# Attention up-projections from one weight chunk, and two output tiles taken together at the start of a stage

## The reference, cut to what matters

```python
def _mixer_mla(b, q_norm_g, w_uq, kv_norm_g, w_ukv, pos):
    c_q, c_kv, k_rope = jnp.split(b, [256, 384], axis=-1)           # latents: 256, 128, rope 32
    q = (_rms_norm(c_q, q_norm_g) @ w_uq).reshape(B, S, 4, 96)      # 4 heads, 64 + 32
    kv = (_rms_norm(c_kv, kv_norm_g) @ w_ukv).reshape(B, S, 4, 128) # keys 64, values 64
    ...                                                             # rope, softmax attention

def second_block(x, ...):
    for l in range(2):
        x = _layer_norm(alpha * x + 0.5 * _swiglu(x, ...), ...)
        x = _layer_norm(alpha * x + _token_mixers(x, ...), ...)     # window, MLA, axial, differential
        x = _layer_norm(alpha * x + 0.5 * _swiglu(x, ...), ...)
    return x
```

## Time and profile before

| | us |
|---|---|
| median of 3 runs (3507.78 to 3513.71) | 3512.36 |
| the profiled execution, its own time | 3510.07 |
| its span, first to last instruction | 3508.3 |
| TensorE busy | 3367.8 |
| VectorE busy | 1803.3 |
| ScalarE busy | 1411.4 |
| mean granted TensorE clock, of full | 0.977 |

### The profile page before, as it was taken

The page is one execution under the profiler, slowest core; times in us unless marked ns, Lnnn a source line. Parts: engine busy times, 40 slices in busy tenths (PEclk is TensorE's granted clock), DMA queues, the critical chain, the costliest instruction groups (busy, mean ns, idle before and its releaser), DMA issues.

```text
span 3508.3 us, 47079 instructions
## 1 busy us (share of the span) xinstructions
PE 3367.8 (96%) x17468; PEld 2774.4 (79%) x17468; DVE 1803.3 (51%) x2572; ACT 1411.4 (40%) x2167; POOL 12.7 (0%) x13
## 2 busy tenths in 40 slices
PE   7999999999999999999998999999999999899997
PEld 6898888888788888888865778888888866588886
DVE  5573566537766534333577553335333576563335
ACT  5323344326544324222456442224232457542223
POOL 0000000001000000000000000000000000000000
PEclk9999999999999999999999999999999999999998
DMA  3201232322232322222211122222223210122233
GB/s 130 67 31 37 80 102 96 99 95 93 76 102 96 99 95 95 97 97 95 76 43 35 43 78 96 98 97 89 96 96 99 80 52 28 35 76 96 96 98 102
DMA packets 89736, 288.48 MB, mean 82 GB/s; under 512 B 9968, under 2 KB 14576, under 8 KB 89072
## 3 DMA queue, kind: packets, MB, share of 16 engines
q1 hardware_dynamic: 89440, 284.69, 24.6%
q0 software_dynamic: 144, 1.71, 0.1%
HBM read 284.26 MB, written 2.10 MB: 82 GB/s over the span
## 4 chain that ended last, share of the span: by engine, by line
PE 84%; DVE 9%; ACT 4%; issue 3%; DMA 1%; DVEq 0%; ACTq 0%; SPq 0%
PE gb L583 24%; PE gb L584 24%; PE gb L585 24%; PE gb L1244 2%; DVE wl L2023 1%; PE pm L1257 1%; PE pm L1277 1%; DVE rinv L2053 1%; ACT wh L1405 1%; ACT h L1455 1%; DMA wst<-in_weights 1%; DVE h L2039 1%; DVE work_a L2656 1%; ACT work_a L1893 1%; ACT xh L1467 0%
## 5 line engine op out<-in xcount | busy, mean ns | idle before, releaser
L583 PE MATMUL gb<-xh,wh 128*128 128x512 f32 (+1 forms) x3168 | 1193.7, 377 | 59.7 <-DVE xl L2077 31.6
L584 PE MATMUL gb<-xl,wh 128*128 128x512 f32 (+1 forms) x3168 | 1169.9, 369 | 0.0
L585 PE MATMUL gb<-xh,wl 128*128 128x512 f32 (+1 forms) x3168 | 1169.8, 369 | 0.0
L2023 DVE TENSOR_TENSOR wl<-wst,wh 128x1024 fp32r<-128x1024 f32 (+3 forms) x600 | 646.5, 1091 | 447.3 <-ACT wh L1405 441.2
L1405 ACT CAST wh<-wst 128x1024 fp32r<-128x1024 f32 (+3 forms) x600 | 555.7, 942 | 604.4 <-DMA wst<-in_weights 604.2
L583 PEld LDWEIGHTS gb<-xh,wh 128*128 128x128 f32 x3168 | 605.7, 191 | 197.4 <-issue 49.9
L584 PEld LDWEIGHTS gb<-xl,wh 128*128 128x128 f32 x3168 | 607.2, 192 | 99.1 <-issue 4.9
L585 PEld LDWEIGHTS gb<-xh,wl 128*128 128x128 f32 x3168 | 606.6, 191 | 98.6
L583 PE MATMUL gb<-hid,wh 128*128 128x512 f32 (+2 forms) x1276 | 471.6, 370 | 10.3 <-DVE wl L2023 9.5
L585 PE MATMUL gb<-hid,wl 128*128 128x512 f32 (+2 forms) x1276 | 467.9, 367 | 0.0
L584 PE MATMUL gb<-hid,wh 128*128 128x512 f32 (+2 forms) x1276 | 467.8, 367 | 0.0
(11 more groups left out here) (401 smaller groups left out, 2989.9 us busy)
## 6 DMA issues: line engine op xcount, KB each, us to landing
wst<-in_weights SPq DMA_DIRECT2D x408, 512.0 KB, 3.3
wst<-in_weights SPq DMA_DIRECT2D x84, 384.0 KB, 3.0
wst<-in_weights SPq DMA_DIRECT2D x84, 320.0 KB, 2.9
h<-in_x_t SPq DMA_DIRECT2D x2, 1024.0 KB, 6.1
out_t<-h SPq DMA_DIRECT2D x8, 256.0 KB, 2.3
tab<-in_first SPq DMA_DIRECT2D x1, 1984.0 KB, 14.9
wst<-in_weights SPq DMA_DIRECT2D x20, 96.0 KB, 2.1
tab<-in_second POOLq DMA_DIRECT2D x1, 1666.0 KB, 7.3
```

The costliest lines, as they stand in the source:

```text
L583: pe.matmul(dst, w_hi, x_hi, start=start, stop=False)
L584: pe.matmul(dst, w_hi, x_lo, start=False, stop=False)
L585: return pe.matmul(dst, w_lo, x_hi, start=False, stop=stop)
L2023: dve.tensor_tensor(wl[:, s, m, a], wst[:, s, m, a], f32(wh[:, s, m, a]), ALU.subtract).then_inc(lo_split, 1)
```

## The change

Chunks 9 to 13 of each second-block mixer become one chunk 9 with 768 columns in half 0 (queries) and 512 in half 1 (keys and values), split at step 21. The output projection moves up to chunks 10 to 13; its first two chunks are split at steps 26 and 31. The parts of the up-projections stay at their steps, read the one chunk, and hand over through a new semaphore `lat_done` or, for the last reader of a half, through `half_done` and `chunk_done`. In `two_by_half` the two tiles of the first chunk are taken together in the first token half, and VectorE splits half 1 of the first chunk after j = 0 (`FIRST_AT`) in place of j = 1.

```diff
-UQ_COLS = (2 * 96, 2 * 96)
+LAT_COLS = (4 * 2 * 96, 4 * 64 + 2 * P)
-M0_C, LRU_C, M2_C = 20, 14, 18
+M0_C, LRU_C, M2_C = 20, 14, 14
+FIRST_AT = 0
-SPLIT_STEP = {0: 3, 3: 4, 6: 5, 10: 6, 14: 7, 18: 8, 21: 9, 24: 10, 25: 11, 27: 12, 28: 13, 30: 14, 32: 15}
+SPLIT_STEP = {0: 3, 3: 4, 6: 5, 10: 6, 14: 7, 18: 8, 21: 9, 26: 10, 31: 11}
...
-                stream(c0 + FF_C + 8, 2, (COLS, COLS), UQ_COLS)
-                stream(c0 + FF_C + 10, 4, UQ_COLS)
-                stream(c0 + FF_C + 14, 4)
+                stream(c0 + FF_C + 8, 2, (COLS, COLS), LAT_COLS)
+                stream(c0 + FF_C + 10, 4)
...
+                def two_tiles(v, s, m, j):
+                    t = HV[v]
+                    if s == 0 and m == 0:
+                        pe.wait_ge(xl_ready, 8 * n + 4 * v + j + 1)
+                    if v == 0 and j == 0:
+                        wait_half(c + s, m)
+                    for k in (2 * j, 2 * j + 1):
+                        col = slice(k * P, k * P + P)
+                        mm = three(gb[:, 2 * s + m, t], wh[:, s, m, col], wl[:, s, m, col], xh[:, k, t], xl[:, k, t],
+                                   k == 0, k == KT - 1)
+                    if v == 1 and j == KT // 2 - 1:
+                        mm.then_inc(chunk_done if m else half_done, 1)
+
+                together = (0, 0), (0, 1), (1, 0), (0, 2), (1, 1), (0, 3), (1, 2), (1, 3)
+                for v in range(2):
+                    for m, j in sorted(together) if v else together:
+                        two_tiles(v, 0, m, j)
+                        if v == 0 and m == 0 and j == 3 and not isinstance(ln_run, str):
+                            sums(n, ln_run, 1)
+                    for m in range(2):
+                        for j in range(KT // 2):
+                            two_tiles(v, 1, m, j)
...
                 def latent_part(c, i):
                     q("ml_lo", 3, 2 if c < 11 else 3)
                     for m in ((i,) if c < 11 else range(2)):
-                        wait_half(c0 + c, m)
+                        wait_half(c0 + 9, 0 if c < 11 else 1)
                         bank_free(c, m)
...
-                        mm.then_inc(chunk_done if m else half_done, 1)
+                        mm.then_inc(half_done if (c, m) == (10, 1) else S("lat_done"), 1)
...
-                        if v == 0 and first and j == 1:
+                        if v == 0 and first and j == FIRST_AT:
                             split_half(*first, 1)
```

More of the change, by code:

```diff
@@ L179, in pack_weights @@
         ukv = i["mla_w_ukv_2"][l].reshape(1, P, 4, 128)
[L180 to L184, removed]
+        up_kv = np.concatenate([ukv[0, :, :, :64].reshape(P, 256), ukv[0, :, :, 64:].reshape(P, 256)], 1)
+        put(uq.transpose(2, 0, 1, 3).reshape(8, P, 96), up_kv.reshape(P, 8, 64).transpose(1, 0, 2))
         w = i["w_out_2"][l].reshape(4, 4, 64, D)
@@ L1195, in latent_part @@
                         for k, f in enumerate(tiles):
-                            col = slice(k * width, k * width + width)
-                            mm = three(gb[0:width, m, :], wh[:, c % 2, m, col], wl[:, c % 2, m, col], *lat(f), k == 0, k == len(tiles) - 1)
-                        mm.then_inc(chunk_done if m else half_done, 1)
+                            at_ = (2 * (2 * (c - 9) + m) + k if c < 11 else 2 * (c - 11) + m) * width
+                            col, half = slice(at_, at_ + width), 0 if c < 11 else 1
+                            mm = three(gb[0:width, m, :], wh[:, 1, half, col], wl[:, 1, half, col], *lat(f), k == 0, k == len(tiles) - 1)
+                        mm.then_inc(half_done if (c, m) == (10, 1) else S("lat_done"), 1)
                 def latent_values(c, m):
-                    wait_half(c0 + c, m)
                     bank_free(c, 1)
+                    cols = slice(256 + P * m, 256 + P * m + P)
                     for t in range(NT):
@@ L1206, in latent_values @@
                         x_hi, x_lo = lat_tok(t)
[L1207 to L1210, removed]
+                        pe.matmul(dst, x_hi, wh[:, 1, 1, cols], start=True, stop=False)
+                        pe.matmul(dst, x_hi, wl[:, 1, 1, cols], start=False, stop=False)
+                        mm = pe.matmul(dst, x_lo, wh[:, 1, 1, cols], start=False, stop=True)
+                    mm.then_inc(chunk_done if m else S("lat_done"), 1)
                 def part_of(c, i):
@@ L1333, in out_part @@
                         for m in range(2):
-                            wait_half(c0 + 14, m)
+                            wait_half(c0 + 10, m)
                         q("exp_done", NS, NS - 1)
@@ L1372, in mixer2 @@
                 q("exp_done", NS, NS)
-                residual_out(c0 + 14, None, n, l, 2 + l, 1)
+                residual_out(c0 + 10, None, n, l, 2 + l, 1)
             def lat(k):
@@ L1473, in norm @@
                     high(j, 0)
-                    if first and j == 0:
+                    if first and j == FIRST_AT:
                         split_half(*first, 1)
@@ L1834, in split @@
                 def split(c):
-                    split_hi(c0 + c, c % 2, UQ_COLS if 9 <= c < 14 else (COLS, COLS))
+                    split_hi(c0 + c, c % 2, LAT_COLS if c == 9 else (COLS, COLS))
                 def evict(c, b):
@@ L1841, in evict @@
                     else:
-                        act.wait_ge(chunk_done if b or c == 13 else half_done, c0 + c + 1)
+                        if c < 9:
+                            act.wait_ge(chunk_done if b else half_done, c0 + c + 1)
+                        elif c == 13:
+                            act.wait_ge(chunk_done, c0 + 10)
+                        elif (c, b) == (10, 1):
+                            act.wait_ge(half_done, c0 + 10)
+                        else:
+                            q("lat_done", 8, 2 * (c - 9) + b + (1 if c < 11 else 0))
                     src = gb[:, 2 * (c == 1) + b, :]
@@ L1979, in mixer2 @@
                         split(SPLIT_STEP[u])
-                residual_out(c0 + 14, n, l, 1)
+                residual_out(c0 + 10, n, l, 1)
             act.wait_ge(S("ones_ready"), 1)
@@ L2633, in split @@
                 def split(c):
-                    split_lo(c0 + c, c % 2, UQ_COLS if 9 <= c < 14 else (COLS, COLS))
+                    split_lo(c0 + c, c % 2, LAT_COLS if c == 9 else (COLS, COLS))
                 def maxima(s):
@@ L2774, in mixer2 @@
                 assert m2.count == M2_STEPS, m2.count
[L2775 removed]
+                residual_out(c0 + 10, 6 + 3 * l, l, 1)
             dve.memset(one[:, :], 1.0)
@@ L2809, in _ @@
                 mixer2(l, c0 + FF_C, 2 + l)
-                norm(n + 1, l, late=(lambda: late_out(c0 + FF_C + 14, n + 1, l), lambda: tail_add(n + 1, 1)), first=(c0 + FF_C + M2_C, 0), split=next_split(c0 + FF_C + M2_C + 1))
+                norm(n + 1, l, late=(lambda: late_out(c0 + FF_C + 10, n + 1, l), lambda: tail_add(n + 1, 1)), first=(c0 + FF_C + M2_C, 0), split=next_split(c0 + FF_C + M2_C + 1))
                 ffn(c0 + FF_C + M2_C, g0 + FF_G + M2_G, 3 + 2 * l, n + 2, l, None)
```

## The result

| | before | after |
|---|---|---|
| median, us | 3512.20 (4 runs) | 3490.42 (3486.76 to 3493.01, 4 runs) |
| profiled execution, its own time | 3510.07 | 3490.86 |
| span | 3508.3 | 3489.1 |
| TensorE busy | 3367.8 | 3355.1 |
| span less TensorE busy | 140.5 | 134.0 |

The account below looks back on a forecast made before the run. TensorE, busy 96% of the span, bounds the kernel; only its idle time and the half clock behind can shrink. 17.6 plus 1.7 gives 19.3 us off 3510.07, 3490.8, put at 3492 against the median; 8-in-10 range 3482 to 3506.

Parts of the forecast that it names:

- Part one: Both second-block mixers: one latent chunk removes waits and half clock, net 8.8 us per layer, 17.6 for two.
- The wait of 4.19 us: Both mixers, part of chunk 12 waiting for its split: wait goes, 4.19 us, plus 3.9 of half clock behind it.
- the 2.71 us wait: Mixers, TensorE behind ScalarE's copy of a transposition, with an output chunk's split just ahead: the 2.71 us goes.
- The split at step 21: Mixers: wider latent halves end 1.4 us later on VectorE, all on TensorE; with 1.5 of half clock, 2.9 lost.
- The two waits ahead of step 28: Mixers, output split at step 26: TensorE waits 1.6 us for an eviction and 0.7 for a rotation, 2.3 lost.
- four waits of 0.3 to 0.6 us: Mixers, step 28 to 33: TensorE runs closer behind VectorE's maxima and ScalarE's copies, 1.8 us lost per layer.
- the stall only moves: Rival: output splits at steps 26 and 31 bring waits with half clock as before; time 3501 us, chance 0.18.
- Part two: Ten first-chunk stages: two tiles together and an earlier VectorE split fill TensorE waits, 1.7 us gained in all.
- The stages pinned to their second half: Five stages behind second-block layer norms: less cover makes a wait 1.4 us longer; 0.5 gained in each of four.
- the later half clock that I charged with 1.0 in all: Part two's stages: longer waits late in a stage bring half clock into TensorE-bound work, 1.0 us lost in all.
- The three stages with sums ahead: Stages at 1317, 2404, 3484 us: moved split delays the late add and sums 1.2 us; 0.3 charged each.
- The slower rival: First halves of ten stages: tile (0, 1) at half clock delays the sums up to 2.6 us; 3519 us, chance 0.06.

Follow-up runs that it names:

- together_rms: Changed kernel with tiles together and early split only in the four stages behind RMS norms, the others as before: 3493.20 us, 0.9939 to the kernel before.
- out_splits_late: Changed kernel with its first two output chunks split at steps 30 and 32 in place of 26 and 31: 3486.10 us, 0.9925 to the kernel before.
- chunk_alone: Changed kernel with the old tile order and VectorE's split of half 1 back after j = 1, leaving the merged latent chunk: 3497.20 us, 0.9956 to the kernel before.
- together_late_split: Changed kernel, tiles still together, with only VectorE's split of half 1 back after j = 1: 3485.45 us, 0.9927 to the kernel before.
- together_alone: Kernel before with two tiles together and the earlier split of half 1, its five latent chunks kept: 3500.81 us, 0.9968 to the kernel before.
- changed_again: Changed kernel, unedited, profiled and timed again: 3490.51 us, 0.9944 to the kernel before.
- latent_split_20: Changed kernel with the latent chunk split at step 20 in place of 21: 3479.06 us, 0.9913 to the kernel before.
- latent20_out24: Changed kernel with the latent chunk split at step 20 and the first output chunk at 24 instead of 26: 3477.65 us, 0.9896 to the kernel before.

## Why the prediction was right, and where its terms were off

**Part one, the mixers: right in mechanism and place, and in the net.** From step 20 to step 39 the sum said 8.8 us a layer; the profiles of the changed kernel show 8.6 to 8.7 four times. Of its single terms:
- The wait of 4.19 us and the half clock behind it went as listed; the 2.71 us wait became 0.82.
- The split at step 21 cost 1.42 us on TensorE, as worked out (1.4). The 1.5 us of half clock that I added for the 2.8 us wait did not come: the clock is 1.00 from 1868 to 1900. It can come: in together_rms the clock is 0.62 from 1868 to 1877, behind the same wait, and 1.3 us are lost by step 24.
- The two waits ahead of step 28 were placed right and sized at 2.3; measured 1.52 and 0.88. From step 28 on I took four waits of 0.3 to 0.6 us, 1.8 in all; the trace has 1.08, 0.79, 0.82, 1.13 and 0.72. This term is too small, and the absent half clock gives back what it loses, which is why the net agrees. That is partly luck.
- One reading was loose: the clock of 0.92 "before the 4.19 us wait" is a mean over 1895 to 1906, which takes in most of the wait. It is 1.00 from 1895 to 1904 and 0.58 from there to 1906, so the clock fell within the wait.
- The edits to the two output splits carry 3.4 of the 8.6 us; out_splits_late shows that.

**The rival "the stall only moves" is partly true, at times.** In chunk_alone's second mixer the same new waits were followed by half clock and the net fell to 5.56 us. In together_late_split it was 6.84 and 2.53, in together_rms 5.45 and 2.49. So the same edit gives 2.5 to 8.7 us a layer, by whether the clock falls behind the waits of 0.8 to 1.5 us at steps 26 to 29. The sum took one outcome for fixed. In the profile of chunk_alone this makes 3.1 us of what is missing from the expected 17.4; the 2.3 us lost before 413, where that kernel has no edit, cover the rest.

**Part two: the term that was mis-sized.** I took 1.7 us; together_alone measured 9.7 by its median, 8.2 by its profile. The step that failed is the walk through the stages, which counted idle time and priced the twelve matmuls of tile (0, 1) at 0.12 us each. The first three rows below are of the kernel before: the wait ahead of the third pair in the stage at 419 us, the low clock behind it, and the low clock in the stage at 2022 us, behind a mixer. The last row is that second place in the changed kernel:

```profile
424.18 0.58 PE L583 MATMUL gb<-xh,wh 128*128 128x256 f32 x1 [1.87 <-DVE xl L2080]
...
425.00:431.00 6.00, 6.00 (x30) 5.56 (x29) 4.41 (x5) 2.00 (x3) 0.00 (x0) 0.60 0.01 3
...
2027.00:2034.00 7.00, 5.38 (x18) 4.64 (x19) 4.06 (x6) 3.91 (x6) 0.00 (x0) 0.50 0.01 2
...
2018.00:2025.00 7.00, 7.00 (x48) 6.60 (x47) 5.13 (x6) 3.94 (x7) 0.00 (x0) 0.94 0.00 0
```

In the changed kernel the wait of 1.87 us is gone: TensorE is at half clock there, the twelve matmuls take 0.213 us each, 2.6 in all, and cover it. The 0.86 us at 420.81 is a new wait, for the second pair, which the moved split delays. Behind it the half clock ends sooner (0.93 from 424 to 430, where it was 0.60), and the stretch from 413 to 784 gains 2.65 to 2.83 us, where I had 0.4 and where the two variants with the old order show 0.5. In the 946 us stage the waits fell from 2.78 to 1.53 us (forecast 1.8), and changed_again gains the 1.0 us of the forecast from 940 to 1310. In the first profile a wait of 1.24 us at 971.73 for VectorE took that back.

**The stages pinned to their second half** behave as told in one point: at 1705.90 and 1707.80 TensorE waits 0.95 and 0.92 us, in place of 0.92 once, so most of the cover of twelve matmuls comes back as waiting. And the later half clock that I charged with 1.0 in all did come in this profile: 0.59 from 1707.8 to 1712, for 2.0 us ahead of the first mixer and 1.7 ahead of the second. In changed_again the same waits stand in the same place with no half clock behind them, and the same stretches gain 0.5 and 1.0. Behind the mixers the stages gain 1.9 to 2.0 each, four times what I took, because the half clock of the stage at 2022 us ends sooner (0.94 from 2018 to 2025).

**The three stages with sums ahead** behave as told: at 2388.75 TensorE waits 1.78 us for the late add, and the loop's turn follows with 3.50 us; nearly nothing of it reaches the next mark (0.0 to +0.6). The stretch from 1310 to 1681 gained 0.9 where I had charged 0.3, but the variants range from -1.3 to +0.4 there with either order, so this can't be put down to the edit.

**The slower rival** needed the sums to come later at half clock by 1.8 us a stage. Relative to the stage's first matmul they came 0.5 us later in the stage at 946 and 2.0 earlier in that at 2022; the rival is refuted by together_alone.

That the total was right within 2 us is in part luck, because two errors cancel in the medians: part one alone gave about 4 us less than its sum of 17.6, part two alone about 8 more than its 1.7. In the pair of profiles the parts stand at 17.3 us for steps 20 to 39, against +3.1 in steps 0 to 20, where no instruction was changed, and -5.0 for the rest.

## What to carry to other kernels

When TensorE's idle gaps are short and many, sum the busy time beside the span: a change that leaves the number of matmuls alone and shrinks busy time has gained clock, and a walk that counts only waits will miss that. Where merged work is prepared matters beside the merging: moving the split from step 21, where it stood ahead of a reciprocal on the critical chain, to step 20 was worth 1.8 us a layer by the trace. Judge an edit of a few us by the stretch it touches, with marks at the same instructions, and not by medians whose runs spread by 16 us.

## What was not expected of the hardware

One wait of about 1.86 us at the same instruction, step 9 of the first mixer, had three outcomes. In both profiles of the changed kernel the clock is 0.54 for the 6 us from the end of the wait, and the scores take 1.77 and 1.70 us. In the kernel before, the scores take 1.13 us, at full rate, and the clock falls 2 us later (0.72 over the same 6 us). In latent_split_20, latent20_out24 and out_splits_late, which up to that step are the same program as the changed kernel, it doesn't fall there. The row and the stretch behind it in latent20_out24:

```profile
1773.49 1.13 PE L1250 MATMUL gb<-work_a 32*128 32x512 f32 x4 [1.86 <-DVE sm L2669]
...
1776.00:1782.00 6.00, 6.00 (x46) 4.18 (x46) 4.40 (x10) 5.79 (x9) 0.00 (x0) 1.00 0.01 3
```

From step 8 to step 12, where nothing was edited, the outcomes ranged from -2.1 to +1.5 us over the profiles. The Trainium skill, TensorE: Matmul & The Clock Gate, The HAM clock gate (the "warmup" mystery), says that the point at which the rate changes varies from run to run; these profiles agree, and show what it is worth here: one program, 3483.8 to 3499.7 us, with mean granted clocks from 0.983 to 0.979.
